# The last expert of an MoE layer: squares moved behind a copy on ACT, six loads moved ahead of two stores on GpSimd

## What is computed

```python
aff = jax.nn.softmax((xf @ w_router).astype(jnp.float32), axis=-1)
gate, idx = lax.top_k(aff.T, cap)                      # cap = 128 tokens for each expert
xe = xf[idx]
hid = jax.nn.silu(einsum(xe, w_gate)) * einsum(xe, w_up)
ye = einsum(hid, w_down) * gate[..., None]
y = jnp.zeros_like(xf).at[idx.reshape(-1)].add(ye)     # summed over the experts
x = x + gate2 * rmsnorm(y, g_post_ffn)                 # the layer's output
```

## Time and profile before

| | us |
|---|---|
| median of 3 runs | 2357.35 (2355.95 to 2357.39) |
| the profiled execution, its own time | 2355.28 |
| its span | 2353.5 |
| PE busy | 2243.9 (95%) |
| DVE, ACT, POOL busy | 1394.8, 1098.6, 752.2 |
| DMA, mean over the span | 217 GB/s |

### The profile page before, as it was taken

How to read it: one execution, slowest core, us unless ns; L and a number is a source line. 1 busy time by engine, 2 the same in 40 slices (tenths; PEclk the granted TensorE clock), 3 DMA queues, 4 the chain that set the end, 5 groups by cost and what they waited for, 6 DMA issues and landing times. The chain is left out here.

```text
span 2353.5 us, 34440 instructions
## 1 busy us (share of the span) xinstructions
PE 2243.9 (95%) x13107; PEld 1865.6 (79%) x13107; DVE 1394.8 (59%) x2067; ACT 1098.6 (47%) x1768; POOL 752.2 (32%) x770
## 2 busy tenths in 40 slices
PE   6999999999999999999983999999999999999996
PEld 4679989867899888676763888888888888888885
DVE  3213344555423436665558877777777878888874
ACT  4212434555434436665542544544444444555552
POOL 3004241434223515341003322212222334544443
PEclk9999999999999999999996999999999999999998
DMA  8735445657554459764537567666667679999995
GB/s 318 266 111 184 153 148 190 191 138 181 144 189 149 152 167 248 211 192 156 187 126 298 210 225 250 226 222 217 227 225 243 227 245 326 316 311 318 327 292 187
DMA packets 224095, 511.47 MB, mean 217 GB/s; under 512 B 38421, under 2 KB 129445, under 8 KB 204497
## 3 DMA queue, kind: packets, MB, share of 16 engines
q1 hardware_dynamic: 174576, 394.78, 49.0%
q0 software_dynamic: 49376, 114.78, 17.9%
HBM read 415.32 MB, written 93.69 MB: 216 GB/s over the span
## 5 line engine op out<-in xcount | busy, mean ns | idle before, releaser
L2562 DVE TENSOR_TENSOR moe_w_lo<-moe_wf,moe_w_hi 128x2048 fp32r<-128x2048 f32 x192 | 436.7, 2287 | 196.2 <-ACT moe_w_hi L2418 195.2
L2418 ACT ACTIVATE moe_w_hi<-moe_wf 128x2048 fp32r<-128x2048 f32 x192 | 365.8, 1915 | 376.1 <-PE moe_acc L2743 361.9
L2743 PE MATMUL moe_acc<-moe_w_hi,moe_x_hi 128*128 128x512 f32 x1024 | 398.7, 389 | 0.9 <-DVE moe_x_lo L2568 0.6
L2743 PE MATMUL moe_acc<-moe_w_hi,moe_x_lo 128*128 128x512 f32 x1024 | 398.4, 389 | 0.0
L2743 PE MATMUL moe_acc<-moe_w_lo,moe_x_hi 128*128 128x512 f32 x1024 | 398.4, 389 | 0.0
L2743 PEld LDWEIGHTS moe_acc<-moe_w_hi,moe_x_hi 128*128 128x128 f32 x1024 | 192.2, 188 | 41.5 <-DVE moe_x_lo L2568 0.8
L2743 PEld LDWEIGHTS moe_acc<-moe_w_hi,moe_x_lo 128*128 128x128 f32 x1024 | 192.2, 188 | 39.9
L2743 PEld LDWEIGHTS moe_acc<-moe_w_lo,moe_x_hi 128*128 128x128 f32 x1024 | 192.2, 188 | 39.8
L1793 PE MATMUL banks<-fr_w_hi,fr_h_hi 128*128 128x256 f32 x768 | 223.2, 291 | 0.0
L2308 POOL DMA_INDIRECT moe_xe<-scratch_h,moe_parts x120 | 193.9, 1616 | 86.2 <-issue 75.7
L1793 PE MATMUL banks<-fr_w_lo,fr_h_hi 128*128 128x256 f32 x768 | 217.0, 283 | 0.0
(11 more groups left out here) (311 smaller groups left out, 4371.9 us busy)
## 6 DMA issues: line engine op xcount, KB each, us to landing
moe_wf<-in_w_expert_gate SPq DMA_DIRECT2D x64, 1024.0 KB, 5.4
moe_wf<-in_w_expert_up SPq DMA_DIRECT2D x64, 1024.0 KB, 5.1
moe_wf<-in_w_expert_down SPq DMA_DIRECT2D x64, 1024.0 KB, 7.0
fr_w_raw<-in_w_units SPq DMA_DIRECT2D x28, 1024.0 KB, 6.7
fr_bias<-in_na_bias SPq DMA_DIRECT2D x16, 1520.0 KB, 11.4
fr_a_w<-in_w_ada POOLq DMA_DIRECT2D x16, 1024.0 KB, 8.3
scratch_qk_t<-fr_stage SPq DMA_DIRECT2D x64, 256.0 KB, 2.5
scratch_vov<-fr_stage SPq DMA_DIRECT2D x96, 128.0 KB, 2.2
```

Of the source, the lines that this page charges most:

```text
L2418: nc.scalar.activation(w_hi[:, q, :, :], wf[:, q, :, :], ACT.Copy).then_inc(w_hi_ready, 1)
L2562: nc.vector.tensor_tensor(w_lo[:, q, :, :], wf[:, q, :, :], w_hi[:, q, :, :].bitcast(F32), ALU.subtract).then_inc(w_lo_ready, 1)
L2743: mm = nc.tensor.matmul(acc[:, j, b, :], x[:, g, k, :], w[:, q, a, h * HALF:(h + 1) * HALF], start=(k == 0 and i == 0), stop=(k == KC - 1 ...
```

## The change

Two edits, both of the last expert. In ACT's stream the squares of units 24 and 25 stand behind the copy of banks 2 and 3 of the turned `hid`. In POOL's stream the stores of units 22 and 23 leave the end of expert 14's body and stand in expert 15's, behind the loads of units 24 and 25 and the four loads of the last rows.

```diff
--- before.py
+++ after.py
@@ -2388,6 +2388,8 @@
                         pool.wait_ge(x_turned, ONE + e * GROUPS)
                         for g in range(GROUPS):
                             load_last(g)
+                        for n in window(e - 1)[2:4]:
+                            store_unit(n)
                     for n in ns:
                         root(n)
                     for n in ns:
@@ -2396,7 +2398,7 @@
                         store_unit(n)
                 if not is_last(e):
                     scatter(e, j)
-                if ns:
+                if ns and not is_last(e, 2):
                     for n in ns[2:4]:
                         store_unit(n)
 
@@ -2488,9 +2490,9 @@
                     split(e, DOWN, range(0, 2))
                     turned_out(0, (h_hi, j), last_h_turned, last_h_hi_ready, range(0, 2))
                     split(e, DOWN, range(2, NP))
+                    turned_out(0, (h_hi, j), last_h_turned, last_h_hi_ready, range(2, BK))
                     for n in ns:
                         square(n)
-                    turned_out(0, (h_hi, j), last_h_turned, last_h_hi_ready, range(2, BK))
                 else:
                     split(e + 1, GATE, range(0, 2))
                     x_out(e + 1, 1 - j)
```

## The result

The change makes the kernel a little slower: 2359.88 us median of 20 runs against 2356.36 of 20 runs of the kernel before, ratio 1.0014, 95% interval 1.0008 to 1.0020, or +3.3 us (1.9 to 4.7). The profiled execution took 2358.29 us with a span of 2356.5.

What follows compares the result with a forecast made beforehand. POOL's chain was taken to bound the end: 4.7 us gained at the loads are given back by waiting about 4 us behind store 22 plus two issues, net +0.9, so median 2357.35 goes to 2358.3; range 2354.6 to 2361.6.

Steps and rivals of the forecast that it cites:

- the course of events to which the prediction gave 0.76: Loads come earlier, but the roots queue behind store 22's landing; the end moves +0.3 or +1.55 us, middle +0.9.
- The end waits for POOL: End of last expert: DVE takes the last half behind POOL's root 26, so an earlier TensorE end gains nothing.
- TensorE's 5.9 us: Last expert: TensorE's stop waiting for `h_lo` costs 3.4 us and the low clock after it 2.5.
- ACT's edit: Squares behind the copy: no stop or low clock, TensorE ends near 2330.7 instead of 2336.6; worth nothing at the end.
- The part removed: POOL ahead of the last loads: unit 24's load, then limited by the scatter, starts at 2307.7, 4.7 us earlier, not 13.
- The holds: DVE's two weight splits hold two of POOL's six load issues, to 2312.05 and 2314.31; the others take 1.25 us each.
- The part added: Store 23 waits ahead of the roots for store 22's landing, taken as 4.4 us; first root at 2323.3 or 2324.6.
- the other case, load 25 held: Unit 25's load is held by DVE's split; store 22 goes at 2318.35, first root at 2324.6, end +1.55 us.
- the first: Rival: TensorE's gain of 5.9 us reaches the end, giving 2351.4 us; chance 0.05.
- The second: Rival: store 22 takes 9.4 us to land; end +5.3 or +6.5 us, 2362.7 to 2363.9; chance 0.07.
- The third: Rival: DVE's splits hold none of POOL's loads; root at 2321.4, end -1.6 us, 2355.7; chance 0.06.
- The fourth: Rival: scatter lands up to 2 us sooner without store 22 in its queue; end -0.9 us, 2356.4; chance 0.06.

Runs made afterwards that it cites:

- the kernel with narrow splits: The change with DVE's last two weight splits cut to one column per row block in place of 1024; 2358.12 us against 2357.58 before, ratio 1.0006.

## Why the prediction was right, and where it was off

The time lies in the range (2354.6 to 2361.6), and the course of events to which the prediction gave 0.76 is what happened. Its size was off: +0.9 us where +3.3 was measured. The absolute figure, 2358.3 against 2359.88, is nearer only because the three runs of before that it starts from lay 1.0 us above the twenty (2357.35 against 2356.36), which was luck; and a range of 7 us is wide for a term of this size.

- **The end waits for POOL: right.** From root 26 to the end it is 17.4 us in every kernel but one, and TensorE's 5.9 us (6.2 as measured from S) reached the end in none.
- **ACT's edit: right inside, wrong at the end.** The copy, the missing stop, the clock and TensorE's end came as worked out. "Worth at the end: nothing by itself, covered by POOL's chain" was wrong: alone it is worth 2.0 us by the medians, 1.9 by the profiles. The mean of unit 24 was an input of POOL's own chain, and the earlier trace rows shows POOL idle for it, 2.50 us ahead of the root. I had that row and read it only as the start of the chain. In the change the wait for store 22 swallows those 2 us.
- **The part removed: right.** Forecast was a load at 2307.7, 1.27 ahead of S; it went 1.40 ahead, so 4.8 us earlier against S than before (forecast 4.7). The scatter was the limit, and the rest of the 13 us did not come free.
- **The holds: right.** Load 25 slipped through, the third and fourth issue took 1.91 and 1.90, store 22 went out 8.09 behind S (forecast 8.13).
- **The part added: the mis-sized term.** "I take 4.4" for the landing of store 22; it was 6.2. POOL stood idle 6.04 us ahead of store 23 and not some 4, and the first root missed its stretch of 2323.3 to 2324.6 (2325.06 with S where it was before). With load 25 slipped through, the prediction's own sum moves the root by +0.3; it moved by 2.0, and the 1.8 us of the landing are that difference. The middle of +0.9 had in it the other case, load 25 held, which did not occur. I had taken the lower bound, for a store alone, and added the 0.8 by which the fifth load lands later than the second. My own rows spoke against it. The fifth load took 6.0 us, so a sixth, issued at 2315.85, lands near 2321.9, and the store behind it would have landed at 2321.5, ahead of it. In the last 150 us of all thirteen traces the transfers issued by POOL whose landing is shown landed in the order of their issue. A store directly behind six loads was to be priced like one more load, at 6 us or more.
- **The rest.** From the root to root 26 the change took 0.4 us more than before (13.4 against 13.0, from the table), a term I had at nothing; 0.3 of it is the landing of the second addition (7.2 us after 6.9), and when the change ran again it was 13.2. The medians moved by 3.5 (and 2.7 on the other occasion), the stretch behind S by 2.35. The difference, up to 1 us, isn't settled; the span ahead of S varies by 3 us between executions (S from 2308.84 to 2311.96), and all but some hundredths of that is there at the second scatter's issue, ahead of every edit.

Of the rivals, the first is refuted (both edits alone: TensorE ends early in each, and the end does not follow). The second had the right mechanism at too high a price: the landing was late, but by 1.8 us over my figure and not 5. The third was refuted by the change's own issues of 1.91 and 1.90 us, and the kernel with narrow splits shows their cause. The fourth was nothing: load 24 started 14.95 to 15.71 us behind the start of the second scatter's issue with store 22 in its old place and 15.05 to 15.18 without it, so the range needed no room for it. The range was right, its middle was too low: two bounds 6 us apart had been answered with a value near the lower end.

## What to carry to other kernels

Before an issue with a wait is moved on an in-order queue, look up what it waits for and how long ago that was issued where it stands, and where it will stand. Of two stores that must land one after the other, the first costs nothing where POOL has to wait for a scatter anyway; the second held up the loads by 4 to 5 us there; and side by side ahead of work that the end needs they cost a full landing. So move the second, and leave the first where its landing is covered. Price a landing by the transfers that were issued just ahead of it, and not by one alone on the queue. An edit that makes an engine off the end's chain finish earlier is still worth what it shortens of that chain's own idle rows; read the bracket of every row in the chain.

## What was not expected of the hardware

- **A store right behind loads on POOL's queue lands late**: 6.2 us after its issue in three executions and 6.4 in a fourth, 7.16 and 5.6 behind two and one loads of `x1` that followed two additions, 5.3 behind the loads of units 24 and 25 alone, 4.4 when 3.4 us lay between the last load's issue and its own, 3.6 alone. The 6.2 and the 4.4 ended at nearly the same time behind S (14.3 and 14.7), as if the loads ahead set it; what in the queue does was not separated.
- **The hold by DVE is decided at the start of an issue.** In seven executions the load of unit 25 began 0.05 to 0.26 us ahead of DVE's split and took 0.95 to 0.97; in one it began 0.06 behind it and took 3.06. A slip of some tenths in the landing of a scatter so moves the root by 1.2 us, as in the two executions of the kernel with store 22 in its old place (9.08 and 10.31).
- **POOL's own small operations are held as well**: a 128 x 1 root took 1.52 us beside DVE's scaling, 0.57 else.
